# Start-up order, zero matmuls and a six-bank PSUM pool in a two-layer hybrid decoder step

## The reference, cut to what matters

```python
for l in range(2):
    x = x + 0.5 * swiglu(rmsnorm(x, norm_ffn1[l]), w_ffn1_gu[l], w_ffn1_down[l])
    x = x + mixer(rmsnorm(x, norm_mix[l]), ...)       # RG-LRU group and GLA group, one out projection
    x = x + 0.5 * swiglu(rmsnorm(x, norm_ffn2[l]), w_ffn2_gu[l], w_ffn2_down[l])
y = rmsnorm(x, norm_final)

def rmsnorm(x, g): return x * rsqrt(mean(x * x, axis=-1) + 1e-6) * g
def swiglu(x, w_gu, w_down):
    gate, up = split(x @ w_gu, 2)                     # 1024 -> 2 x 2816
    return (silu(gate) * up) @ w_down                 # 2816 -> 1024
```

## Time and profile before

| | |
|---|---|
| runs | lowest 2657.85 us, median of three 2662.12 us |
| profiled execution | 2658.01 us; span of its slowest core (0) 2656.5 us |
| spans of the 8 cores | 2641.7 to 2656.5 us; mean granted TensorE clock 0.991 to 0.995 |
| busy on core 0 | PE 96%, weight loads 59%, DVE 60%, ACT 43%, POOL 25% |
| DMA | 201.79 MB written by the queues, mean 76 GB/s |

### The profile page before, as it was taken

How to read it: one execution, slowest core, us unless ns; L and a number is a source line. 1 busy time by engine, 2 the same in 40 slices (tenths; PEclk the granted TensorE clock), 3 DMA queues, 4 the chain that set the end, 5 groups by cost and what they waited for, 6 DMA issues and landing times.

```text
span 2656.5 us, 51887 instructions; the slowest of 8 cores (2641.7 to 2656.5 us)
## 1 busy us (share of the span) xinstructions
PE 2549.8 (96%) x16788; PEld 1575.5 (59%) x16788; DVE 1586.7 (60%) x3263; ACT 1140.5 (43%) x2090; POOL 660.0 (25%) x1065
## 2 busy tenths in 40 slices
PE   6999989999999999999999999999999999999997
PEld 3566555666666666566556655555665666655654
DVE  4444866665876665544554467665667666574435
ACT  3121556563656663211311135665546666342113
POOL 1311422212512123311321143222243111241110
PEclk9999999999999999999999999999999999999999
DMA  7745345444434352544443533444553343534543
GB/s 190 111 75 79 48 72 88 73 76 75 68 57 81 57 89 47 82 72 65 75 85 52 91 63 50 80 70 79 82 78 51 59 68 63 87 60 86 78 84 93
DMA packets 105381, 201.79 MB, mean 76 GB/s; under 512 B 11936, under 2 KB 15136, under 8 KB 105120
## 3 DMA queue, kind: packets, MB, share of 16 engines
q0 software_dynamic: 95184, 171.25, 41.5%
q1 hardware_dynamic: 9936, 27.22, 3.0%
HBM read 355.92 MB, written 13.71 MB: 139 GB/s over the span
## 4 chain that ended last, share of the span: by engine, by line
PE 80%; ACT 7%; issue 4%; DVE 4%; DMA 2%; POOL 2%; DVEq 0%; ACTq 0%; POOLq 0%; SPq 0%
PE ps L661 43%; PE ps L682 21%; PE ps L764 7%; PE ps L1119 5%; PE ps L944 2%; DMA ring<-wpages 1%; DVE x L686 1%; ACT L672 1%; ACT sg L672 1%; POOL fr L612 1%; DMA S0b<-S 1%; ACT L1034 1%; PE ps L818 1%; ACT fq L604 0%; ACT L620 0%
## 5 line engine op out<-in xcount | busy, mean ns | idle before, releaser
L661 PE MATMUL ps<-xn,ring 128*128 128x366 bf16 (+1 forms) x8448 | 1417.9, 320 | 39.8 <-ACT sg L672 22.4
L661 PEld LDWEIGHTS ps<-xn,ring 128*128 128x128 bf16 x8448 | 817.3, 98 | 550.3 <-issue 73.5
L682 PE MATMUL ps<-h,ring 128*128 128x366 bf16 (+1 forms) x4224 | 708.9, 319 | 15.7 <-DMA ring<-wpages 5.9
L686 DVE SCALAR_TENSOR_TENSOR x<-ps,x 128x366 f32<-128x366 f32 (+1 forms) x1152 | 587.9, 536 | 157.7 <-PE ps L682 112.8
L576 POOL DMA_DIRECT2D ring<-wpages x644 | 345.4, 541 | 1282.3 <-PE ps L661 692.8
L672 ACT ACTIVATE sg<-ps 128x366 f32<-128x366 f32 (+1 forms) x528 | 248.7, 475 | 892.3 <-PE ps L661 811.3
L674 DVE TENSOR_TENSOR h<-ps,sg 128x366 bf16<-128x366 f32 (+1 forms) x528 | 282.0, 536 | 572.2 <-PE ps L661 433.7
L682 PEld LDWEIGHTS ps<-h,ring 128*128 128x128 bf16 x4224 | 406.1, 98 | 258.9 <-issue 31.3
L764 PE MATMUL ps<-XN,ring 128*128 128x366 bf16 (+1 forms) x1536 | 269.2, 319 | 4.6 <-ACT ra L820 1.2
L604 ACT ACTIVATE fq<-x 128x366 bf16<-128x366 f32 (+1 forms) x240 | 117.9, 505 | 205.2 <-DVE x L1122 100.9
L764 PEld LDWEIGHTS ps<-XN,ring 128*128 128x128 bf16 x1536 | 147.2, 98 | 97.7 <-issue 13.9
(11 more groups left out here) (148 smaller groups left out, 1709.1 us busy)
## 6 DMA issues: line engine op xcount, KB each, us to landing
ring<-wpages POOLq DMA_DIRECT2D x644, 256.0 KB, 5.8
x<-xT SPq DMA_DIRECT2D x10, 732.0 KB, 7.7
yT<-x SPq DMA_DIRECT2D x10, 732.0 KB, 3.4
S0f<-S SPq DMA_DIRECT2D x16, 256.0 KB, 3.1
Sos<-S0f SPq DMA_DIRECT2D x16, 256.0 KB, 2.2
S0b<-S POOLq DMA_DIRECT2D x16, 128.0 KB, 4.6
x<-xT SPq DMA_DIRECT2D x4, 362.0 KB, 7.4
yT<-x SPq DMA_DIRECT2D x2, 724.0 KB, 3.2
```

The lines of the kernel that those rows point to most:

```text
L661: mms = [(lambda h, kc=kc, pg=pg, bk=bk: h.matmul(psum[bk.bank][:, :n], lhsT=pg.a[:, kc * 128:(kc + 1) * 128], rhs=xb.b[:, kc * n:(kc + 1) ...
L682: pe([(lambda h, jj=jj, j=j, mc=mc, bD=bD: h.matmul(psum[bD.bank][:, :n], lhsT=pgs[j, 2].a[:, mc * 128:(mc + 1) * 128], rhs=hs_[jj].b[:, : ...
L686: dve(lambda h, mc=mc, bD=bD: h.scalar_tensor_tensor(out=xa(ti, mc), in0=psum[bD.bank][:, :n], scalar=0.5, in1=xa(ti, mc), op0=ALU.mult, o ...
```

## The change

It does five things.

- `POOLS`: the FFN pool becomes banks 0 to 3, 6 and 7, the same six as `ANY_POOL`.
- Norms of the first SwiGLU of half A: only tile 0 stays on PE; tiles 1 and 2 have their squares added on DVE. `warm` puts matmuls on zeros (`XN[0]`, into bank 5) into PE's list: 5 after every second square of tile 0, 14 after the last, 29 in all. An Ln on ones, on ACT, is entered at the start; the memsets of the mixer's buffers move from `setup` to the start.
- Pages 2 to 11 read the second piece of x, `("x", 2, 0)`. The load of tile 1 is cut into four and names `("pg", 3)`, that of tile 2 names `("pg", 9)`.
- The gate and up chains of tile 0 in the fourth group (g == 3) write a mark `("from", q)` for the tiles of half B, which the squares of a norm read: B's first norm waits for them.
- The planner's costs: a page 1400 instead of 1750, SP's loads at 250 instead of 180 bytes per ns, the memsets of XN 1300 instead of 300.

```diff
-POOLS = ((0, 1, 2, 3), (3, 4, 5), (0, 1, 2, 3, 6, 7))
+POOLS = ((0, 1, 2, 3, 6, 7), (3, 4, 5), (0, 1, 2, 3, 6, 7))
...
-            return P.add("sp", fn, reads, writes, dma_sem=sem, cost=80.0, nbytes=nbytes / 180.0)
+            return P.add("sp", fn, reads, writes, dma_sem=sem, cost=80.0, nbytes=nbytes / 250.0)
...
-                      dma_sem=page_sem[s], cost=540.0, nbytes=1750.0)
+                      dma_sem=page_sem[s], cost=540.0, nbytes=1400.0)
...
+        def warm(k):
+
+            pe([lambda h: h.matmul(psum[5][:, 0:366], lhsT=ones[:], rhs=XN[0].b[:, 0:366], start=True, stop=True)] * k,
+               XN[0].k + ["ones"], [PB((5,))], mm_ns(366, k))
...
-        def norm(ti, gcol, dst, dkey, which, on_pe=False):
+        def norm(ti, gcol, dst, dkey, which, on_pe=False, first=False, on_dve=False):
...
+            add2 = dve if on_dve else pool2
...
-                act(lambda h, kc=kc, q=q: h.activation(out=q.b[:, :n], in_=xa(ti, kc), func=AF.Square), [("x", kc, ti)], q.k, n)
+                act(lambda h, kc=kc, q=q: h.activation(out=q.b[:, :n], in_=xa(ti, kc), func=AF.Square), [("x", kc, ti), ("from", ti)], q.k, n)
...
+                    if first and kc % 2:
+                        warm(14 if kc == KC - 1 else 5)
...
-                    pool2(lambda h: h.tensor_tensor(out=r.f[:, :n], in0=q0.b[:, :n], in1=q1.b[:, :n], op=ALU.add),
+                    add2(lambda h: h.tensor_tensor(out=r.f[:, :n], in0=q0.b[:, :n], in1=q1.b[:, :n], op=ALU.add),
...
-                     lambda kc, b=b: b.k[kc], "f", on_pe=base == 0 and half[0] == 0)
+                     lambda kc, b=b: b.k[kc], "f", on_pe=base == 0 and t == 0, first=base == 0 and t == 0, on_dve=base == 0 and half[0] == 0)
...
-                    unit(js, t, base, pgs)
+                    unit(js, t, base, pgs, [("from", q) for q in B] if base == 0 and half[0] == 0 and t == 0 and g == 3 else [])
...
-                        pe(mms, [pg.k] + xb.k, [bk], mm_ns(n, KC))
+                        pe(mms, [pg.k] + xb.k, [bk] + mark, mm_ns(n, KC))
...
         load_x(0, parts=4)
+        act(lambda h: h.activation(out=sm[:, SPT:SPT + 4], in_=ones[:, 0:4], func=AF.Ln), ["ones"], ["spt"], 4, tbl="ln")
+        for b in XN + [gb["ks"] for gb in gbuf]:
+            P.add("dve", lambda h, b=b: h.memset(b.f[:, :], 0.0), (), b.k, cost=1300.0 if b in XN else 250.0)
...
         for i in range(2, 12):
-            start_after[i] = [("x", 4, 0)]
-        load_x(1, [("x", 6, 0), ("pg", 7)])
-        load_x(2, [("x", 4, 1), ("pg", 11)])
+            start_after[i] = [("x", 2, 0)]
+        load_x(1, [("x", 6, 0), ("pg", 3)], parts=4)
+        load_x(2, [("x", 4, 1), ("pg", 9)])
```

More of the change, by code:

```diff
@@ L607, in norm @@
                                                       start=(kc == 0), stop=(kc == KC - 1)), q.k + ["ones"], [ps], mm_ns(n))
+                    if first and kc % 2:
+                        warm(14 if kc == KC - 1 else 5)
                 elif kc == 1:
-                    pool2(lambda h: h.tensor_tensor(out=r.f[:, :n], in0=q0.b[:, :n], in1=q1.b[:, :n], op=ALU.add),
+                    add2(lambda h: h.tensor_tensor(out=r.f[:, :n], in0=q0.b[:, :n], in1=q1.b[:, :n], op=ALU.add),
                           q0.k + q1.k, r.k, n)
                 elif 1 < kc < KC - 1:
-                    pool2(lambda h, q=q: h.tensor_tensor(out=r.f[:, :n], in0=r.f[:, :n], in1=q.b[:, :n], op=ALU.add),
+                    add2(lambda h, q=q: h.tensor_tensor(out=r.f[:, :n], in0=r.f[:, :n], in1=q.b[:, :n], op=ALU.add),
                           q.k + r.k, r.k, n)
                 elif kc == KC - 1:
-                    pool2(lambda h, q=q: h.tensor_tensor(out=q0.b[:, :n], in0=r.f[:, :n], in1=q.b[:, :n], op=ALU.add),
+                    add2(lambda h, q=q: h.tensor_tensor(out=q0.b[:, :n], in0=r.f[:, :n], in1=q.b[:, :n], op=ALU.add),
                           q.k + r.k, q0.k, n)
@@ L645, in ffn, with unit @@
                         ffn_norm(t)
-                    unit(js, t, base, pgs)
-        def unit(js, ti, base, pgs):
+                    unit(js, t, base, pgs, [("from", q) for q in B] if base == 0 and half[0] == 0 and t == 0 and g == 3 else [])
+        def unit(js, ti, base, pgs, mark):
             n = TILES[ti][1]
@@ L734, in setup @@
                         op0=ALU.mult), ["cols"], ["hb"])
[L735 to L739, removed]
         acount = [0, 0, 0]
@@ L1126, in build_program @@
         load_x(0, parts=4)
+        act(lambda h: h.activation(out=sm[:, SPT:SPT + 4], in_=ones[:, 0:4], func=AF.Ln), ["ones"], ["spt"], 4, tbl="ln")
+        for b in XN + [gb["ks"] for gb in gbuf]:
+            P.add("dve", lambda h, b=b: h.memset(b.f[:, :], 0.0), (), b.k, cost=1300.0 if b in XN else 250.0)
+        for gb in gbuf:
+            for nm in ("qa", "qb"):
+                P.add("dve", lambda h, gb=gb, nm=nm: h.memset(gb[nm].f[:, :], 0.0), (), gb[nm].k, cost=280.0)
         for i in range(2, 12):
-            start_after[i] = [("x", 4, 0)]
-        load_x(1, [("x", 6, 0), ("pg", 7)])
-        load_x(2, [("x", 4, 1), ("pg", 11)])
+            start_after[i] = [("x", 2, 0)]
+        load_x(1, [("x", 6, 0), ("pg", 3)], parts=4)
+        load_x(2, [("x", 4, 1), ("pg", 9)])
         for t in B:
```

## The result

The changed kernel takes 2629.6 us (median of four runs, 2627.8 to 2635.1), 0.987 of the kernel before, 95% interval 0.983 to 0.992. The forecast was 2642 us, range 2618 to 2670, no change by 2%. The time fell in the range, on its fast side; the two terms of the sum were wrong in opposite directions.

The account below looks back on a forecast made before the run. PE, busy 2549.8 of 2656.5 us, was taken as the bound, its 106.7 us idle capping reordering apart from slow matmuls. From 2658 us, 8 for the start and 8 for six banks gave 2642 us, range 2618 to 2670.

Parts of the forecast that it names:

- the two terms of the sum: Whole kernel: the start and the six banks, 8 us gained each, taken from 2658 us.
- Bound and size of the whole: Whole kernel: reordering regains at most PE's 106.7 us idle, plus slow matmuls' cost; faster by 2% has chance 0.04.
- First chain, +0.4 us: Tile 0's first chain at the start: 0.4 us later, as the last piece of x meets pages; bounds 0 and +1.4.
- Zeros, 0: Start: the 29 zero matmuls mostly run free where PE waits, cost 0 to 1.3 us, gain nothing; taken as 0.
- Pages 3 and 9: Start: page 3 sent at 29.2 us, landing near 40; page 9 sent near 38 to 39, landing at 44 to 50.
- Tile 1's first chain at 34.9: Start: tile 1's first chain at 34.9 us instead of 39.62, with DVE's sums running as pieces land.
- Start, -8: First 100 us: loss falls from 43.8 to 35.7 us, gaining 8; bounds 18 gained, 5 lost.
- Six banks, -8: Gate and up chains' Silu waits outside the mixed stretches: 8 us gained, bound -18; nothing in the mixed ones.
- Rival (b): Mixed stretches: gate and up chains in banks 6 and 7 delay GLA's outputs, up to 2705 us; chance 0.14.
- Rival (a): Start gives nothing because page 3 comes late; the banks' 8 remain or vanish: about 2656 us; chance 0.18.
- (c): Whole kernel: start gains its 18 us and nearly all 20.5 us of Silu waits go: 2622 us; chance 0.10.
- Costs move no page, waits for pages stay: Planner's cheaper DMA costs: page slots free as before, and down chains' 5.9 us of waits for pages stay.

Follow-up runs that it names:

- `no_zeros`: The changed kernel without the 29 matmuls on zeros; two runs, 2629.4 and 2634.9 us.
- `setup_late`: The changed kernel with the table set-up (two Exp on ACT, six scalings on DVE) waiting for the fourth group's mark; 2628.7 us, 0.989 of the kernel before.
- `third_piece`: The changed kernel with pages 2 to 11 behind the third piece of x again; 2623.2 to 2632.0 us, 0.989 of the kernel before.
- `pages_late`: `setup_late` with the ten mixer pages also waiting for the fourth group's mark; 2621.9 us, 0.987 of the kernel before.
- `four_banks`: The changed kernel with gate and up chains back in four banks, all else kept; 2660.0 us, 1.001 of the kernel before.
- `banks_only`: The kernel before with only gate and up chains allowed six PSUM banks; 2630.7 to 2636.0 us, 0.991 of the kernel before.
- `old_costs`: The changed kernel with the planner's DMA costs of before (page 1750, loads at 180 bytes per ns); median 2628.9 us, 0.989 of the kernel before.

## Why the prediction was right or wrong

- **Bound and size of the whole.** That PE's idle time caps the gain and a change by 2% is out of reach held: 13.4 us of idle went and 9.5 of busy time, and the ratio is 0.987. That 2% is about what a measurement tells from none was too cautious: the interval, 0.983 to 0.992, lies clear of 1. That the time fell in the range is in part luck: the sum gave the start and the banks 8 us each, and an error of 8 in the one hid part of an error of 16 to 22 in the other.
- **First chain, +0.4 us: wrong, 2.55.** The last piece of x was 0.3 us late, as said (0.8 and 1.0 in `no_zeros` and `setup_late`, which load in the same order). The step that failed is that I followed only x past the earlier pages. The constants go out on the same queue behind x and were there at 15.9 us (13.2 in the kernel before); an Exp that I had not looked for waits for them on ACT ahead of the norm, and DVE's set-up stands ahead of the scalings (`third_piece` shows the constants' part, `setup_late` the set-up's).
- **Zeros, 0: right.** They ran where PE waits, as said, and were over at 9.6 us, so it is not they that make the first chain later than 19.5, which was named as a sign of being wrong. One reading was incomplete: the 3.1 us by which tile 0's first matmuls are slow were not all DVE's pace. Before, the first eight start 0.51 us apart, which makes 2.5, and five more 0.30 apart, at half pace, which makes the rest. So a higher clock could have gained 0.6 us there, but the one that the zeros raised had fallen again (last section). By the trace the early Ln and the memsets cost nothing either: the third piece's squares still wait for x.
- **Pages 3 and 9: nearly right.** They went out at 30.45 and 38.01 us (29.2 and 38 to 39 said). PE never waited for page 3 (1.4 us said), as it came there later. The first down chain came at 53.69, not 49.
- **Tile 1's first chain at 34.9: wrong, 40.80.** Its squares start at 30.17, but then wait for DVE's sums, two buffers at a time:

```profile
30.17 0.90 ACT L610 ACTIVATE fq<-x 128x366 bf16<-128x366 f32 x2
32.39 0.91 ACT L610 ACTIVATE fq<-x 128x366 bf16<-128x366 f32 x2 [1.32 <-DVE fr L617]
33.70 1.16 ACT L610 ACTIVATE fq<-x 128x366 bf16<-128x366 f32 x2 [0.41 <-DVE fr L620]
35.02 1.15 ACT L610 ACTIVATE fq<-x 128x366 bf16<-128x366 f32 x2 [0.16 <-DVE fr L620]
```

 I had the sums run as pieces land. The planner put the squares behind tile 0's third Silu, which ends at 30.3, so all eight were worked off after that, though the tile's pieces landed one after another until 30.45.
- **Start, -8: wrong, about 0.** 3.8 us at 80 us, of which none is left at 300, and the banks have a part in those: between kernels with the same banks the new start is 1.0 to 1.7 us ahead at 80 us and 3.2 to 3.6 behind at 300. The terms that failed are the first chain and tile 1's norm, above, and one that the sum left out: I stopped it at the first down chain and did not ask what the earlier PE meets next, the second group's pages, sent in POOL's list among ten mixer pages. `pages_late` shows that part; `four_banks` shows the end, 1.001 of before.
- **Six banks, -8: wrong, -24 to -30** (`banks_only`: 0.991 of before; after against `four_banks`: 2629.6 against 2660.0). The step that failed is "In the mixed ones GLA's outputs hold 6 and 7 [...]: nothing". Waits for Silu went there too, from 10.5 us to 1.5, in `banks_only` to 5.6. At 2300 us `banks_only` is 20.1 us ahead of before, 8.0 of it from the mixed stretches, and the changed kernel 20.0 ahead of `four_banks`, 10.7 of it from them (-3.1 from the first, 13.8 from the second). Outside them the term was too small as well: 12.1 and 9.3 us. That two banks used by others part of the time are of no use to a chain of 2 us was an argument, not a reading.
- **Rival (b), slower through GLA: fell.** GLA's first matmuls into banks 6 and 7 wait 1.2 us in all from 300 to 2300 us for the copy of the state (before: 1.0, and 0.9 for another input of theirs), and in the profiled core's list of waits never for a Silu or a product of an FFN. **Rival (a)** was right about the start, though not by its reason, since page 3 held nothing, and wrong about the end; **(c)** came closest in size, 2622 against 2629.6, with the wrong split.
- **Costs move no page, waits for pages stay: wrong.** They rose by 8 us (5.9 to 14.1) and fell back with the old costs (4.2 in `old_costs`), without a change of the time. The 5.9 of the earlier trace rows was the highest of the eight cores.

## What to carry to other kernels

When a wait is removed at the start of a long pipeline, follow the gain to the first resource that the earlier work meets; here 3.8 us were given back within 220 us. When a transfer is moved ahead, list every transfer on the queues it passes, the small ones too, and what waits for them in an engine's fixed order. Buffers that an engine uses only part of the time are worth lending: two PSUM banks removed two thirds of the waits for Silu by themselves (22.4 to 7.1 us), some of them in the stretches where others use these banks as well. And read from the trace what an edit did: the edit that put pages behind tile 1 also made the planner send tile 1 itself 9.5 us sooner.

## What the runs showed of the hardware

The 68 KB of constants suffered more from the earlier pages than a 362 KB piece of x sent just before them. Their load in the changed kernel and in `third_piece` (the last number is the time from issue to landing):

```profile
cols_sb<-cols SPq DMA_DIRECT2D x1, 68.0 KB, 12.9
```

```profile
cols_sb<-cols SPq DMA_DIRECT2D x1, 68.0 KB, 10.2
```

The last piece of x was squared at 13.44 us instead of 13.12.

The 29 zeros take 6.60 us where 29 x 0.156 + 0.16 = 4.7 would do at full pace: PE starts at the lower of its two clocks. The loads of their weights start 0.30 us apart at first, and 0.15 from 6.9 us on:

```profile
6.31 0.15 PEld L595 LDWEIGHTS ps<-XN,ones 128*128 128x128 bf16 x1 [0.15 <-issue]
6.62 0.15 PEld L595 LDWEIGHTS ps<-XN,ones 128*128 128x128 bf16 x1 [0.15 <-issue]
6.92 2.31 PEld L595 LDWEIGHTS ps<-XN,ones 128*128 128x128 bf16 x15 [0.15 <-issue]
```

Windows of the changed kernel's trace (the column after the engines is the granted clock) show how long this lasted:

```profile
0.00:7.00 7.00, 4.00 (x14) 2.02 (x15) 4.95 (x10) 2.39 (x4) 1.40 (x6) 1.00 0.65 132
7.00:13.80 6.80, 4.16 (x23) 2.01 (x21) 0.24 (x2) 2.16 (x5) 4.22 (x8) 1.00 0.98 205
13.80:20.20 6.40, 0.86 (x2) 0.21 (x2) 3.01 (x16) 2.02 (x7) 0.00 (x0) 0.50 1.06 190
20.20:27.40 7.20, 6.83 (x20) 2.62 (x21) 5.24 (x16) 1.76 (x2) 0.00 (x0) 0.50 1.04 234
27.40:33.40 6.00, 5.92 (x38) 3.53 (x36) 1.32 (x3) 2.64 (x6) 0.53 (x1) 0.99 1.03 235
```

From 9.6 to 13.8 us PE did only six sums of squares; then the clock was granted at half, and it still was when the first chain began. So the zeros bought that chain no pace. Without zeros:

```profile
20.60:26.60 6.00, 5.62 (x16) 2.02 (x17) 4.72 (x15) 1.76 (x2) 0.00 (x0) 1.00 1.03 221
```

This window reads 1.00, and yet its last matmuls start 0.30 us apart, at half pace. The 1.00 there, and in the first window above, says nothing of the pace: the trace's records of the clock begin only at 26.65 us in this run and at 6.99 us in the changed kernel, each time when the matmuls go over to full pace, and a stretch without a record reads 1.00. At the start of a trace the duration of the matmuls says at what pace PE goes.
